# Both experts' gate and up products ahead of both down products, the gather in two halves, and two gain loads at other places

## The reference, cut to what matters

```python
def moe(u, w_router, b_router, w_gate_up, b_gate_up, w_down, b_down):
    t = u.reshape(B * L, D)                       # D = 1024
    logits = (t @ w_router + b_router)
    vals, idx = lax.top_k(logits, TOP_K)          # 4 of 32
    comb = ...                                    # softmax of the four, 0 for the others
    for e in range(N_EXPERTS):                    # 32
        gu = t @ w_gate_up[e] + b_gate_up[e]      # 1024 x 2048
        gate = jnp.minimum(gu[:, :D_EXPERT], SWIGLU_LIMIT)
        up = jnp.clip(gu[:, D_EXPERT:], -SWIGLU_LIMIT, SWIGLU_LIMIT)
        h = (up + 1.0) * (gate * jax.nn.sigmoid(SWIGLU_ALPHA * gate))
        out = out + comb[:, e:e + 1] * (h @ w_down[e] + b_down[e])   # 1024 x 1024
ple = rmsnorm(p @ w_ple[i], g_ple_post[i]) * jax.nn.sigmoid(rmsnorm(x, g_ple[i]) @ w_ple_gate[i])
x = x + ple                                       # then rmsnorm(x, g_final)
```

## Time and profile before

| | us |
|---|---|
| three runs, median | 1236.56 |
| lowest, highest | 1235.95, 1239.75 |
| the profiled execution, its own time | 1239.27 |
| span of the profiled execution (first to last instruction) | 1237.5 |
| PE busy (share of the span) | 1181.4 (95%) |
| DVE, ACT, POOL busy | 316.5, 210.5, 30.4 |
| moved by DMA | 447.40 MB, 362 GB/s over the span |
| first and last weighing of gate/up (L1087) | 263.0, 1173.2 |

### The profile page before, as it was taken

The page is one execution under the profiler, slowest core; times in us unless marked ns, Lnnn a source line. Parts: engine busy times, 40 slices in busy tenths (PEclk is TensorE's granted clock), DMA queues, the critical chain, the costliest instruction groups (busy, mean ns, idle before and its releaser), DMA issues.

```text
span 1237.5 us, 14451 instructions
## 1 busy us (share of the span) xinstructions
PE 1181.4 (95%) x5795; PEld 575.0 (46%) x5795; DVE 316.5 (26%) x786; ACT 210.5 (17%) x416; POOL 30.4 (2%) x67
## 2 busy tenths in 40 slices
PE   7999999999999999999999999999999999899987
PEld 5777777553443434344343434343434343434333
DVE  4445204241222122122212121222222121211133
ACT  2555502120110100010100011110100000000024
POOL 1000200000000000000000012000000000000000
PEclk9999999998999999999999999999999999999999
DMA  9833763479899999999999999999999999999941
GB/s 302 289 136 136 225 272 136 177 277 393 352 428 428 427 428 428 427 430 426 432 426 430 427 428 426 406 428 427 427 428 427 428 429 428 425 428 427 427 201 39
DMA packets 51762, 447.40 MB, mean 362 GB/s; under 512 B 8126, under 2 KB 9374, under 8 KB 26904
## 3 DMA queue, kind: packets, MB, share of 16 engines
q1 hardware_dynamic: 48896, 440.30, 86.1%
q0 software_dynamic: 2704, 6.36, 1.7%
q10 hardware_dynamic: 112, 0.03, 0.0%
HBM read 445.16 MB, written 1.88 MB: 361 GB/s over the span
## 4 chain that ended last, share of the span: by engine, by line
PE 72%; DMA 24%; ACT 2%; DVE 1%; POOL 1%; issue 1%; SPq 0%; DVEq 0%; ACTq 0%
PE ps L1087 23%; DMA ring<-in_w_gate_up 22%; PE ps L765 16%; PE ps L1105 13%; PE ps L958 6%; PE ps L1121 3%; PE ps L910 2%; PE ps L1209 2%; DMA out<-work 2%; PE ps L1045 1%; PE ps L1035 1%; POOL out L729 1%; PE ps L795 1%; PE ps L759 1%; DMA x_tok<-in_x_prompt 0%
## 5 line engine op out<-in xcount | busy, mean ns | idle before, releaser
L1087 PE MATMUL ps<-ring,work 128*64 128x512 f32 x2016 | 443.5, 593 | 22.0 <-DMA ring<-in_w_gate_up 21.7
L1087 PEld LDWEIGHTS ps<-ring,work 128*64 128x64 f32 x2016 | 143.6, 137 | 302.7 <-issue 250.6
L1105 PE MATMUL ps<-ring,work 128*64 128x512 f32 x1024 | 230.3, 603 | 5.9 <-ACT work L1429 5.1
L765 PE MATMUL ps<-work,ring 128*128 128x288 f32 x752 | 186.2, 409 | 0.0
L765 PEld LDWEIGHTS ps<-work,ring 128*128 128x128 f32 x752 | 143.5, 191 | 41.4 <-issue 1.7
L1105 PEld LDWEIGHTS ps<-ring,work 128*64 128x64 f32 x1024 | 72.0, 139 | 145.8 <-issue 132.7
L1952 DVE TENSOR_SCALAR work<-ps 128x512 f32<-128x512 f32 x32 | 22.1, 692 | 394.8 <-PE ps L1087 394.8
L958 PEld LDWEIGHTS ps<-work,x_tok 128*128 128x128 f32 x768 | 91.9, 196 | 13.5 <-issue 12.6
L958 PE MATMUL ps<-work,x_tok 128*128 128x128 f32 x768 | 95.4, 284 | 0.4 <-DVE work L1811 0.4
L1484 ACT ACTIVATE work<-work 128x512 f32<-128x512 f32 x32 | 20.2, 630 | 439.9 <-DVE work L1952 439.9
L1811 DVE TENSOR_SCALAR work<-iota_slot,slot,stat 128x64 f32<-128x64 f32 x96 | 24.4, 311 | 222.3 <-PE ps L1105 222.3
(11 more groups left out here) (259 smaller groups left out, 604.6 us busy)
## 6 DMA issues: line engine op xcount, KB each, us to landing
ring<-in_w_gate_up SPq DMA_DIRECT2D x126, 2048.0 KB, 29.4
ring<-in_w_down SPq DMA_DIRECT2D x64, 2048.0 KB, 33.5
ring<-in_w_in SPq DMA_DIRECT2D x7, 2048.0 KB, 14.6
ring<-in_w_proj_b SPq DMA_DIRECT2D x2, 2048.0 KB, 7.7
ring<-in_w_proj_a SPq DMA_DIRECT2D x2, 2048.0 KB, 10.6
ring<-in_w_out SPq DMA_DIRECT2D x2, 2048.0 KB, 9.8
ring<-in_w_ple_gate SPq DMA_DIRECT2D x4, 1024.0 KB, 30.4
ring<-in_w_in SPq DMA_DIRECT2D x2, 1024.0 KB, 9.1
```

The lines of the kernel that those rows point to most:

```text
L765: mm = pe.matmul(out(b), lhs, rhs, start=(k == 0), stop=(k == len(pairs) - 1))
L1087: mm = pe.matmul(ps[half(g), b, :], xg[:, k, i % 2, :], block(k % 2, at + 512 * g), start=False, stop=(k == KC - 1))
L1105: mm = pe.matmul(ps[half(g), b, :], hT[:, 4 * j + k, :], whole_piece(s)[:, at + 512 * g:at + 512 * g + 512], start=False, stop=(4 * j + k ...
```

## The change

- **Order on PE.** In a pair: gate/up of the first expert, `add_pair`, gate/up of the second with the first's `turn_hidden` after two of its eight steps, down of the first with the second's `turn_hidden` in its middle, the transposes of `sel_w`, half of `gather`, half of the second's down, the other half of `gather`, the other half of down. There are two places for the turned hidden rows, `hT_of`: the old one, and part of `o_pair` for the first expert.
- **Order of the pieces.** `STREAM` lists it: 4 + 4 pieces of gate/up, then 2 + 2 of down. The two extra pieces are now the first expert's down weights.
- **PSUM banks.** `CHUNK` gives bank, uses in a pair and place for each use: gate (both) and the second hT in bank 0, up in bank 1, the first hT and out (both) in bank 2.
- **DVE and ACT** follow: all of `select_tile` at a pair's start, `swiglu` twice, the second `pick_d` after the first expert's output, the copy of gathered inputs at the end. `scale_embedding` comes before the second SwiGLU of pair 9.
- **Gains.** The broadcast of `g_ple_post` is issued by POOL once the first expert's output sums are there, ahead of `w_ple`; its four small loads stay where they were. All of `g_final` is issued after the four quarters of `w_ple_gate` have landed (`t_landed`).

```diff
+STREAM = [(2 * j + s, q) for j in range(2) for qs in (range(GU_PIECES), range(GU_PIECES, PIECES))
+          for s in range(2) for q in qs]
...
+        hT_of = [o_pair[:, 0:512].rearrange("p (c s) -> p c s", s=CAP), hT]
...
-            chunk_filled(pool, "up", 1)
+            chunk_filled(pool, "out", 0, 0)
+            pool.dma_start(g_post, g_ple_post[0:1, :].partition_broadcast(P)).then_inc(g_post_landed, 16)
             pool.dma_start(wple, w_ple[0].rearrange("(k p) c -> p k c", p=P)).then_inc(p_landed, 16)
...
-            load_gains(g_post, g_post_q, g_ple_post[0:1, :], g_post_landed)
+            load_gain_quarters(g_post_q, g_ple_post[0:1, :], g_post_landed)
             pool.wait_ge(squares[2], TT)
-            load_gains(g_last, g_last_q, g_final.rearrange("(a d) -> a d", a=1), g_last_landed)
+            pool.wait_ge(t_landed, 16 * 4)
+            pool.dma_start(g_last, g_final.rearrange("(a d) -> a d", a=1).partition_broadcast(P)).then_inc(g_last_landed, 16)
+            load_gain_quarters(g_last_q, g_final.rearrange("(a d) -> a d", a=1), g_last_landed)
...
             def quad(Q, late, embeds=False, last=False):
...
+                for j in range(2):
+                    m, i = Q * 2 + j, 2 * j
+                    first = isinstance(m, int) and m == 0
+                    later = late or (embeds and j == 1)
+                    begin_gate_up(m, 0)
...
+                    weigh_gate_up(Q, i, m, later)
...
+                    if not first:
+                        add_pair(m, later)
+                    if embeds and j == 0:
                         turn_tails()
-                    if embeds and i == 1:
+                    begin_gate_up(m, 1)
+                    weigh_gate_up(Q, i + 1, m, later)
+                    if embeds and j == 0:
                         embed()
...
+                    begin_down(m, 0)
+                    weigh_down(Q, i, 0)
+                    turn_hidden(m, 1)
+                    weigh_down(Q, i, 1)
+                    turn_pair_weights(m)
+                    if not (last and j == 1):
+                        gather(m + 1, 0, late or embeds)
+                    begin_down(m, 1)
+                    weigh_down(Q, i + 1, 0)
+                    if not (last and j == 1):
+                        gather(m + 1, 1, late or embeds)
+                    weigh_down(Q, i + 1, 1)
```

More of the change, by code:

```diff
@@ L428, in place, with extra_piece, wait_expert_piece @@
             return at % SLOTS, Q * (QUAD_PIECES // SLOTS) + at // SLOTS
[L430 to L436, removed]
+        def extra_piece(Q, i, q):
+            x = STREAM.index((i, q)) - SLOTS
+            return x if isinstance(Q, int) and Q == 0 and 0 <= x < EXTRAS else None
+        def wait_expert_piece(eng, Q, i, q):
+            x = extra_piece(Q, i, q)
+            if x is not None:
+                eng.wait_ge(extra_landed[x], 16 * (2 + x))
+                return extra_blocks[x]
+            s, turn = place(Q, i, q)
+            eng.wait_ge(piece_landed[s], turn * 16 + 16)
+            rows = whole_piece(s)
+            return [rows[:, D * k:D * k + D] for k in range(4)]
         def own_quarter(q):
@@ L1505, in _ @@
+                    nc.scalar.copy(sel_wT.rearrange("p t s -> p (t s)"), ps[:, B_S, 0:TT * P]) \
+                        .then_inc(emptied[B_S], 1)
+                    if begins and j == 0:
+                        copy_residual()
+                    keep_output(m, 1, share=ends and j == 1)
             quad(0, begins=True)
@@ new lines, in quad @@
+            def quad(Q, e0, late, embeds=False, ends=False):
+                for j in range(2):
+                    m, n, e = Q * 2 + j, Q * 4 + 2 * j, e0 + 2 * j
+                    first, final = isinstance(m, int) and m == 0, ends and j == 1
+                    if not first:
+                        chunk_filled(dve, "out", m - 1, 1)
+                    if not final:
+                        for t in TILES:
+                            last = select_tile(t, n + 2)
+                        last.then_inc(sel_ready, 1)
+                    pick_expert(pick_d[:], e, scaled=True).then_inc(pick_d_ready, 1)
+                    for q in range(2):
+                        for t in range(TT):
+                            last = V.tensor_scalar(sel_w[:, t, CAP * q:CAP * q + CAP], iota_slot[:],
+                                                   column(slot, t, n + q), column(comb, t, e + q),
+                                                   ALU.is_equal, ALU.mult)
+                    last.then_inc(sel_w_ready, 1)
+                    swiglu(m, 0)
+                    pick_expert(pick_gu, e + 1).then_inc(pick_gu_ready, 1)
+                    if not first:
@@ L1970, in quad @@
                             mean(2, P, slice(0, 2))
-                        add_pair(m, late or (embeds and i == 2))
-                    if i % 2 == 1 and not (ends and i == 3):
+                        add_pair(m, late or (embeds and j == 1))
+                    if embeds and j == 1:
+                        scale_embedding()
+                    swiglu(m, 1)
+                    if not final:
+                        pick_expert(pick_gu, e + 2).then_inc(pick_gu_ready, 1)
+                    chunk_filled(dve, "out", m, 0)
+                    pick_expert(pick_d[:], e + 1, scaled=True).then_inc(pick_d_ready, 1)
+                    if not final:
                         gathered(m + 1, late or embeds)
```

292 lines of the change are left out of this document (131 added, 161 removed).

## The result

| | before | changed |
|---|---|---|
| median of six runs, us | 1237.10 | 1229.28 |
| lowest, highest | 1235.95, 1239.75 | 1227.47, 1231.87 |
| profiled execution: its own time, span | 1239.27, 1237.5 | 1230.32, 1228.6 |

The ratio of the changed kernel to the kernel before is 0.9933, with a 95% interval of 0.9921 to 0.9945: some 8 us less. The forecast was 1228.3 us, and its range holds the measured time.

What follows compares the result with a forecast made beforehand. The stream of expert weights, about 428 GB/s, was taken to bound the kernel, not PE. Start, gain loads and tail sum to -1.5 - 3.9 - 2.9 = -8.3 us, from median 1236.56 to 1228.3 us; range 1225.5 to 1230.5, chance 66.

Steps and rivals of the forecast that it cites:

- Part 1: First pair, the stream's start: slot released at 315.8 instead of 318.9, 1.5 us idle again; gain 1.5 us.
- The price of the low clock: First pair, PE after the SwiGLU wait: half of 283.1 to 289.5 charged as lost, 3.2 us.
- rival B: Start gives more: clock returns sooner since dense work starts 1.5 us earlier; 1.5 to 3 us, 1225.3 to 1226.8; chance 7.
- Part 2: Gain loads taken out of the full stream: 3.5 to 4.3, taken 3.9 us; remaining small loads cost 0.3 or 1.1.
- Part 3: Tail: only 16 instructions, 3.55 us, plus hand-over follow the last piece; ACT at 1186.7, gain 2.9 us.
- Rival C: Tail's gain is taken by w_ple_gate's last quarter; margin 1.2 us, price up to 2.9: 1231.2; chance 7.
- Part 4: Middle pairs: PE takes at most 54.9 us, under the stream's 58.8; embedding's wait doesn't empty the ring; gain nothing.
- 58.8 - 54.9: Pairs after the embedding: DMA time of a pair minus PE's, so PE wins back 3.9 us or more in each of seven.
- by pair 14: Sign after the embedding: PE catching up with the stream, chain through DMA, by pair 14.
- its 4.6: Embedding in quad 4: PE 26.9 us behind a landing where 31.5 is allowed, so the ring has 4.6 us to spare.
- rival D: Slower: embedding's wait empties the ring once the last store lands 4.6 us later, each further us costing one; chance 8.
- Rivals A: Start gives nothing: PE later in pair 0, g_ple_post meets a busy stream; price 2.7 up to 4.2, 1231 to 1232.5; chance 12.

Runs made afterwards that it cites:

- 12 memsets: 12 memsets of an unread 128x256 tile on POOL ahead of quad 4's state stores, added to the changed kernel: 1233.17 us, ratio 0.9958.

## Why the prediction was right, and where it was not

**Part 1 (start), forecast 1.5, trace 2.4.** The mechanism was right: slot by slot as forecast, about 1 us sooner. The price of the low clock was mis-sized for this execution. I charged 3.2 us; the row shows 4.82 us for 16 products that take 3.60 at full clock, 1.06 for 0.62 at the biases, 1.7 us in all. In the four other traces in which the clock fell it is 1.5 to 1.6 us in three and 3.1 in one, so 3.2 was the upper end. And the clock is not certain to fall: of the nine traces with this order and a wait of 2.83 us it fell in five. That is also half of rival B (clock back sooner, 1.5 to 3 us): its mechanism exists, and moves single executions by about 2 us. On g_ple_post: the gap was not closed but shallow, and whether its 1.2 us were covered is open. The rule of the Trainium skill (DMA: Bandwidth & Descriptors, Rules for kernel authors) that transfers of several engines run interleaved on the same 16 DMA engines is borne out by the other load: in the full stream g_final, issued by POOL, cost its bytes and more (2.2 us for 1.5).

**Part 2 (gains), forecast 3.9 (3.5 to 4.3), trace 3.4, alone 3.0.** At the low end. The whole of the first sag stayed, and with it the four small loads: the eight pieces from 763 to 803 us take 40.3 us where eight at 4.9 take 39.2, so 1.1 us are lost, the upper of the two prices named (no run takes the four loads out, so that they cause it isn't shown). That `g_final` comes in time was right, with more room than thought: issued from 1187.8 to 1190.3, the last of it is there at 1193.6, and the reader comes at 1197.7. The Trainium skill (DMA: Bandwidth & Descriptors, Anatomy of one DMA) gives about 2.0 us plus the bytes at 436 GB/s, an estimate of 3.2 us for 512 KB; the trace has 3.5 with the engines empty and agrees. The four small loads took a median of 3.1 us there and of 12.8 in the full stream, which the page's formula does not cover.

**Part 3 (tail), forecast 2.9, trace 3.1.** Right in each step: 3.7 us from the last piece to ACT, pg products at 1188.4, so 8.8 us before those of the earlier trace rows, with `w_ple_gate` in by 1187.2, a margin of 1.2 us. Rival C was as near as stated, and didn't decide.

**Part 4 (the pair in the middle), forecast nothing, trace nothing.** The result was right, but one step under it was wrong, and that it did no harm was luck.

The wait ended as forecast, at 764.8 (765.5), and the last down piece was used at 790.7 (790.4), 27.7 us behind its landing (26.9). It was 8.3 us long and not about 12, since PE reached it at 756.4 and not at 753.2.

Wrong was *"PE wins back 58.8 - 54.9 = 3.9 us or more in each of the seven pairs left"*. A pair takes PE 55.1 us and not at most 54.9, so it wins 3.7; and the first one behind the embedding takes 59.2 and wins next to nothing. In it PE waits 2.0 us for DVE and runs `add_pair` at low clock:

```profile
807.59 5.40 PE L1135 MATMUL ps<-work 128*128 128x512 f32 x8 [2.01 <-DVE stat L1785]
```

Those 8 products take 3.70 us elsewhere. A later stall of PE (3.2 us at 1073, behind it a window at 0.69 of the clock; 2.5 us before) took more. So PE caught up with the very last piece, by 0.28 us, and not by pair 14. Even by the forecast's own figures seven pairs win back 27.3 us, against a lag of 26.9: 0.4 us to spare, which the forecast never set beside its 4.6.

That is also what was wrong with the point of decision of rival D: *"from the point where the last store lands 4.6 us later"*. It looks for the delay that empties the ring. For the slots behind the wait the room was as forecast: the piece issued at 790.72 lands 12.6 us later, 5.0 above the shortest. The tightest slot comes one pair later, in the piece issued at 817.18, with 3.0 (both in this order):

```profile
DMA to landing us min/median/max: 12.6/12.6/12.6
```

```profile
DMA to landing us min/median/max: 10.6/10.6/10.6
```

But a delay must also be made up before the end, and PE had 0.3 us for that. So the 4.65 us of the 12 memsets, of which the ring alone should have taken most, cost 2.5 us in the span, 3.2 counted from the piece at 763 us. That it was not all of 4.65 fits too: POOL began 1.4 us sooner there (733.74 against 735.14), so the last store landed 3.4 us later, and when PE released the last slot of the pair it was 3.1 us later (793.8 against 790.7). Rival D was right in kind (with 11.3 us of delay the changed kernel is slower than before, the kernel before hardly cares, and moving the embedding takes nearly all of it away), but not in its mechanism: by the changed kernel's two traces PE's loss begins at about 0.3 us of delay and not at 4.6, and its 8 in 100 were worked out from the wrong room. In the median it cost nothing: with the embedding moved away the kernel takes the same time.

**Rivals A and C** are out: the start gave its gain, the tail gave its own.

**The sum.** Forecast -1.5 - 3.9 - 2.9 = -8.3. In the traces -2.4 - 3.4 - 3.1 = -8.9; the medians say -7.8 in one group and -8.7 in another. The errors of the first two terms, 0.9 too little and 0.5 too much, partly offset each other: that the total came within 1 us is luck in part.

## What to carry to other kernels

When a stream bounds a kernel, cost a change in three places only: when the stream becomes continuous, what else travels in it, and what follows its last byte; those three terms added up here, as far as runs that differ by some 2 us can tell. An engine that falls behind a stream has two limits, not one: the slots of the ring, at the wait and for a pair behind it, and the time in which it must catch up before the end. Add up what it really wins in each pair that is left, and set it beside the lag; in the trace, look for its first wait for data after the stall. Here that was the very last piece, so any further delay of PE reaches the end, whatever room the ring has left. And when an engine waits for a buffer, look at which instruction frees it: here the last reader stood behind a wait that it didn't need, and moving it was worth 2.3 us.

## What the runs showed of the chip that was not expected

- The same wait of PE (2.83 us, same place, same work around it) lowers the granted clock in some executions and not in others: over 280 to 285 us it is 0.60 to 0.78 in five traces and 1.00 in four. Behind the low clock the 20th weight piece lands at 329.7 to 330.6 us; behind the full one at 328.0, 328.1 and 330.1, and at 326.4 without the broadcast of g_ple_post. A wait of 0.89 us left the clock up in both traces that have it. The Trainium skill (TensorE: Matmul & The Clock Gate, What's actually happening) says that the low clock is the default state and that activity releases it, and that the number of slow products at the start of a kernel varies from run to run; these traces show the clock down behind a wait and up again under work, and such a variation behind a wait inside a kernel. The price of such a wait is therefore a spread, here 0 to 3.1 us of PE and in most traces some 2 us of the landings behind it.
- A chain of memsets of 128x256 on POOL takes 0.36 us for each (4.36 us for 12, 10.99 for 30), so it makes a delay of a chosen length.
- A load of four times 32 KB goes with a loss in the full stream that is larger than its bytes: 0.13 MB, 0.3 us of data, and 1.1 us lost over the eight pieces around it. No run leaves it out, so that it is the cause isn't shown.
